# The doubling levels of the delta rule: each 128-column product as two column tiles of 64

## The chip, the cores and the metric

One NeuronCore of a Trainium2 chip (trn2) runs the whole program. The metric is the device time of one execution in microseconds. Engines are called by their names: TensorE (PE in the profile, PEld for its weight loads), VectorE (DVE), ScalarE (ACT), GpSimd (POOL), SyncE (SP).

## What is computed

The reference is one layer of a hybrid encoder for 512 tokens of 1024 channels, in fp32: a layer norm, a mixer with three branches, and a mixture of experts with 32 experts. The change lies in branch (A), the gated delta rule in both directions, 4 heads of 128 channels. In the reference it goes chunk by chunk:

```
m = where(strict, einsum(kb, k) * decay, 0)
a_mat = m + eye
sol = triangular_solve(a_mat, [v * beta, kb * exp(gc)])
...
v_new = u_n - w_n @ state
state_next = state * exp(gl_n) + kd_n^T @ v_new
```

The kernel uses chunks of 128 tokens. It inverts the unit triangular matrix a_mat itself: first its diagonal blocks of 8 by 8, and then by doubling, with blocks of 8, 16, 32 and 64 joined to blocks of twice the size. Joining blocks costs two products for each level, direction, chunk and head: Y = (off-diagonal part) times (inverse so far), and T = T - (inverse so far) times Y.

## The kernel before, in words

The program has four parts with a barrier of all engines between them: `front` (norm, input projection, gates), `mlstm`, `deltanet`, and `back` (merging of the branches, output projection, router, experts).

`deltanet` (from line 1034) treats 8 batches, m = 0 to 7: two directions by four chunks of 128 tokens. Batches 2p and 2p+1 (called a and b) are worked side by side, one of each direction. The order of the steps is written out by hand in the list `order` (lines 1098 to 1124) and each engine walks the same list. For each pair and each of the four levels l it has: y1(a), y1(b), some steps of other batches, p2(a), p2(b), and, but for the last level, again(a), again(b). Step "y1" multiplies the masked matrix `ot` by half of the columns of `tn` (64 of 128, those of one side of each block) into the lower half of the PSUM bank `lv[d]`; ScalarE copies this to `y1s` (line 1440). Step "p2" multiplies `y1s` by half of the columns of `tt` into the upper half of the same bank; VectorE subtracts it from `tt` (line 1547). Step "again" transposes `tt` afresh (line 1323) and ScalarE writes `tn` (line 1436). GpSimd clears `y1s` and masks the next `ot` (lines 1604 and 1608). Line 1289 is the product that solves the 8 by 8 blocks; it waits for VectorE's line 1520.

Between these steps `order` puts matmuls that don't belong to the delta rule: the list `fill` (lines 1128 to 1144), products of the merge gates (line 1250, 128 stationary columns, 512 streamed, split fp32r, three products for each block) and of the other branches (line 1259, plain fp32). They are dealt out by the dictionary `weight`: as the weights of the steps add up, a like share of the fill list is inserted. The weight of y1, p2 and again counts only for odd m, so that a and b follow directly on one another and fill comes behind b. All fill belongs to this part; at its end the engines meet at the barrier, and `back` starts with its loads.

In the program a product is one call. In the trace a plain fp32 product is two weight loads and two matmuls, so the 4 heads of one y1 step are 8 pairs. The two edited lines are 1308 ("y1") and 1316 ("p2").

Two other lines are spoken of for their shape: line 2176 in `back` adds up a small table with 64 stationary columns (8 products, 32 streamed columns), and line 1886 is the second product of the experts, 64 stationary columns and 512 streamed. Lines 1858 and 1859 are the experts' first products with the full 128 columns.

Of the kernel before, what the change touches and what calls it, by code (L numbers as in the profile page):

```python
# [1033 lines left out]
def deltanet(nc, sem, sb, pb, cn, v):  # L1034
# [9 lines left out]
    with st:  # L1044
# [3 lines left out]
        mt, tt, tn, at, qe = (four(name, 4) for name in ("mt", "tt", "tn", "at", "qe"))  # L1048
        ot, rhs = four("ot", 2), four("rhs", 2)
# [6 lines left out]
        y1s = four("y1s", 2)  # L1056
# [15 lines left out]
        lv = [pb(st, f"lv{i}") for i in range(2)]  # L1072
# [85 lines left out]
        def halves(ap, l, side):  # L1158

            return ap.rearrange("p h (n s b) -> p h n s b", s=2, b=LEVELS[l])[:, :, :, side, :]  # L1160

        def packed(bank, part, l):

            return bank[:, 256 * part:256 * part + 256].rearrange("p (h n b) -> p h n b", h=NH, b=LEVELS[l])
# [27 lines left out]
        with nc.Block() as block:  # L1192
# [47 lines left out]
            def _(pe):  # L1240
                for op in order:
                    if op[0] == "fill":
                        what, c, r, k = op[1:]
                        if what == "gate":
# [4 lines left out]
                            for a, b in PRODUCTS:  # L1249
                                last = pe.matmul(fill_bank(what, c, r)[:, :], gw_part[g % 2][a][:, k, :], h_part[b][:, k, :],  # L1250
                                                 start=(k == 0 and a + b == 0), stop=(k == KT - 1 and a == 1))
# [12 lines left out]
                    d, t = BATCH[m]  # L1264
                    tri = cn("upto" if d == 0 else "after")
                    if kind == "gram":
                        if m >= 1:
                            pe.wait_ge(at_ready, m)
                            pe.wait_ge(kk_used, m)
                        if m % 2 == 0 and m >= 2:  # L1270
                            pe.wait_ge(tn_copied, m)
                        for h in range(NH):
                            last = pe.matmul(pr[0][:, tile(h)], gg[:, t, 4 * d + h:4 * d + h + 1].to_broadcast([P, P]), tri,
                                             start=True, stop=True)
                        last.then_inc(gr_done, 1)
                        for h in range(NH):
                            last = pe.matmul(pr[1][:, tile(h)], qkT[:, 1, h, tile(t)], qkT[:, 1, h, tile(t)],
                                             start=True, stop=True)
                        last.then_inc(kk_done, 1)
                    elif kind == "attn":  # L1280
                        pe.wait_ge(dif_ready, m + 1)
                        pe.wait_ge(egr_ready, m + 1)
                        for h in range(NH):
                            last = pe.matmul(pr[0][:, tile(h)], qkT[:, 1, h, tile(t)], qkT[:, 0, h, tile(t)],
                                             start=True, stop=True)
                        last.then_inc(qk_done, 1)
                    elif kind == "base":
                        pe.wait_ge(spread, m + 1)
                        pe.matmul(pr[1][:, :], cn("block"), facts[:, 0:2 * NH * BASE * BASE],
                                  start=True, stop=True).then_inc(base_done, 1)  # L1290
                    elif kind == "turn":
                        pe.wait_ge(tt_ready, m + 1)
                        if m % 2 == 1:
                            pe.wait_ge(tn_copied, m)
                        for h in range(NH):
                            last = pe.transpose(pr[1][:, tile(h)], tt[:, m % 4, h, :], ident)
                        last.then_inc(turn_done, 1)
                    elif kind == "y1":
                        l = op[2]
                        i = at_level(m, l)  # L1300
                        pe.wait_ge(ot_ready, i + 1)
                        pe.wait_ge(tn_copied, m + 1)
                        if i >= 2:
                            pe.wait_ge(t_updated, i - 1)
                        if l > 0:
                            pe.wait_ge(again_copied, at_again(m, l - 1) + 1)
                        for h in range(NH):
                            last = pe.matmul(packed(lv[d], 0, l)[:, h], ot[:, i % 2, h, :],  # L1308
                                             halves(tn[:, m % 4, :, :], l, d)[:, h], start=True, stop=True)
                        last.then_inc(y1_done, 1)  # L1310
                    elif kind == "p2":
                        l = op[2]
                        pe.wait_ge(y1_copied, at_level(m, l) + 1)
                        pe.wait_ge(y1_cleared, at_level(m, l) + 1)
                        for h in range(NH):
                            last = pe.matmul(packed(lv[d], 1, l)[:, h], y1s[:, d, h, :],  # L1316
                                             halves(tt[:, m % 4, :, :], l, 1 - d)[:, h], start=True, stop=True)
                        last.then_inc(p2_done, 1)
                    elif kind == "again":
                        l = op[2]  # L1320
                        pe.wait_ge(t_updated, at_level(m, l) + 1)
                        for h in range(NH):
                            last = pe.transpose(lv[d][:, tile(h)], tt[:, m % 4, h, :], ident)  # L1323
                        last.then_inc(again_done, 1)
                    elif kind == "norm":
                        n = m - NB // 2
                        pe.wait_ge(osq_done, n + 1)
                        pe.wait_ge(o_taken, m + 1)
                        if m < NB - 2:
                            pe.wait_ge(s_updated, m + 1)  # L1330
                        for h in range(NH):
                            last = pe.matmul(sc[m % 2][:, h:h + 1], mt[:, m % 4, h, :], ones[:, 0:1], start=True, stop=True)
                        last.then_inc(osum_done, 1)
                    elif kind == "root":
                        n = m - NB // 2
                        pe.wait_ge(orec_done, n + 1)
                        for h in range(NH):
                            last = pe.matmul(sc[m % 2][:, tile(h)], root_col[:, n, h:h + 1].to_broadcast([P, P]), ident,
                                             start=True, stop=True)
                        last.then_inc(ospread_done, 1)  # L1340
                    elif kind == "read":
                        if m >= 2:
                            pe.wait_ge(s_updated, m - 1)
                        else:
                            pe.wait_ge(s_zero, m + 1)

                        if m >= NB // 2 + 2:
                            pe.wait_ge(ospread_used, m - NB // 2 - 1)
                        for h in range(NH):
                            last = pe.matmul(sc[m % 2][:, tile(h)], qkT[:, 1, h, tile(t)], state[:, d, h, :],  # L1350
                                             start=True, stop=True)
                        last.then_inc(ks_done, 1)
                    elif kind == "solve":
                        pe.wait_ge(r_ready, m + 1)
                        pe.wait_ge(t_updated, at_level(m, NL - 1) + 1)
                        for h in range(NH):
                            last = pe.matmul(sc[m % 2][:, tile(h)], tt[:, m % 4, h, :], rhs[:, d, h, :], start=True, stop=True)
                        last.then_inc(tr_done, 1)
                    elif kind == "write":
                        pe.wait_ge(vn_ready, m + 1)  # L1360
                        pe.wait_ge(at_ready, m + 1)
                        pe.wait_ge(qe_ready, m + 1)
                        for h in range(NH):
                            pe.matmul(sc[m % 2][:, tile(h)], vn[:, d, h, :], at[:, m % 4, h, :], start=True, stop=False)
                            last = pe.matmul(sc[m % 2][:, tile(h)], state[:, d, h, :], qe[:, m % 4, h, :], start=False, stop=True)
                        last.then_inc(o_done, 1)
                        if m < NB - 2:
                            pe.wait_ge(o_taken, m + 1)
                            for h in range(NH):
                                last = pe.matmul(sc[m % 2][:, tile(h)], kTok[:, t, h, :], vnd[:, d, h, :], start=True, stop=True)  # L1370
                            last.then_inc(ds_done, 1)
# [1233 lines left out]
```

## Time and profile before

| | |
|---|---|
| Time, median of 3 runs | 1304.32 us (1302.6 to 1304.48) |
| Span of the profiled execution, first to last instruction | 1295.8 us |
| Median above that span | 8.5 us |
| TensorE busy | 1218.8 us, 94% |
| TensorE weight loads busy | 854.9 us, 66% |
| VectorE, ScalarE, GpSimd busy | 788.6, 618.9, 171.6 us |
| Mean granted TensorE clock | 0.983 |
| Delta rule stage | 270 to 617 us |

The page has no time of its own for the profiled execution beyond its span; the runs shown are separate executions, and the last rows of the table put the two side by side. "Busy" counts matmuls from start to a modelled end, and since matmuls overlap, the distance between their starts tells more than their length. In the timeline one row stands for successive instructions of one line: its start, the time from the first start to the last end, and their number (x). The shape 128*64 means 128 rows and 64 stationary columns; what is behind it is the streamed operand.

### The profile page before, as it was taken

The numbers are of one execution on the slowest core, as the hardware profiler recorded it, in microseconds if no ns is written. First come the engines' busy times: TensorE is split into PE (matmuls) and PEld (weight loads), VectorE is DVE, ScalarE is ACT, GpSimd is POOL, SyncE is SP. The second block draws the span as 40 slices with busy tenths as digits, with TensorE's granted clock in tenths as the row PEclk, the third lists the DMA queues.
The fourth block names the chain that finished last, engine by engine and source line by source line (L and its number), as shares of the span: only waits on it lengthen the run. The fifth ranks groups of instructions, "written<-read, shape, count | busy, mean of one in ns | idle before, by whom it ended". The sixth has DMA issues, their size and how long they took to land.

```text
span 1295.8 us, 14828 instructions
## 1 busy us (share of the span) xinstructions
PE 1218.8 (94%) x5610; PEld 854.9 (66%) x5610; DVE 788.6 (61%) x999; ACT 618.9 (48%) x815; POOL 171.6 (13%) x178
## 2 busy tenths in 40 slices
PE   5999998989999999999897699999999999999996
PEld 4788876767778787877376555666666665555552
DVE  6687753764343444424655667766666666666676
ACT  6354445664324233232322455666666666666652
POOL 1000160022223123120000110111111111111000
PEclk9999999999999999999999699999999999999999
DMA  7323421162212202211935799999999999999951
GB/s 248 99 72 106 148 66 41 35 220 70 76 42 66 81 27 72 65 42 57 336 126 210 269 410 344 385 405 400 405 404 403 397 399 400 401 392 396 397 212 67
DMA packets 98175, 284.72 MB, mean 220 GB/s; under 512 B 8917, under 2 KB 58709, under 8 KB 72880
## 3 DMA queue, kind: packets, MB, share of 16 engines
q1 hardware_dynamic: 92992, 274.94, 56.5%
q0 software_dynamic: 4960, 8.22, 1.9%
q8 instruction: 48, 0.79, 0.3%
q10 hardware_dynamic: 144, 0.52, 0.1%
q14 instruction: 31, 0.25, 0.1%
HBM read 269.13 MB, written 22.56 MB: 225 GB/s over the span
## 4 chain that ended last, share of the span: by engine, by line
PE 68%; DVE 5%; issue 2%; ACT 2%; DMA 1%; SPq 0%; POOLq 0%; ACTq 0%; DVEq 0%
PE yb L1886 17%; PE fill_ps L1250 10%; PE hb L1858 9%; PE hb L1859 9%; PE fill_ps L1259 3%; PE tx L1842 2%; PE hb L2118 2%; PE lv L1308 2%; PE lv L1316 2%; PE gb L1873 1%; PE gb L1866 1%; PE yb L2118 1%; DMA wraw<-kept_dram 1%; PE lv L1323 1%; DVE wo_lo L2280 1%
## 5 line engine op out<-in xcount | busy, mean ns | idle before, releaser
L1979 DVE TENSOR_TENSOR wlo<-wraw,whi 128x2048 fp32r<-128x2048 f32 x127 | 285.4, 2287 | 30.3 <-ACT whi L1920 30.3
L1920 ACT ACTIVATE whi<-wraw 128x2048 fp32r<-128x2048 f32 x128 | 241.1, 1909 | 35.3 <-PE hb L1859 35.3
L1886 PE MATMUL yb<-wraw,act_t 128*64 128x512 f32 x512 | 227.8, 598 | 6.0 <-issue 6.0
L1858 PE MATMUL hb<-whi,xs 128*128 128x512 f32 x512 | 211.8, 414 | 1.8 <-DVE xs L1983 1.5
L1859 PE MATMUL hb<-wlo,xs 128*128 128x512 f32 x512 | 202.5, 396 | 0.0
L1886 PEld LDWEIGHTS yb<-wraw,act_t 128*64 128x64 f32 x512 | 67.8, 137 | 140.6 <-issue 138.8
L1250 PE MATMUL fill_ps<-h_part,gws 128*128 128x512 f32 x576 | 158.5, 416 | 1.8 <-DVE gws L1472 1.8
L1858 PEld LDWEIGHTS hb<-whi,xs 128*128 128x128 f32 x512 | 97.6, 191 | 45.8 <-issue 25.7
L369 PE MATMUL pj<-h_part,wsplit 128*128 128x512 f32 x528 | 126.0, 397 | 0.0
L1250 PEld LDWEIGHTS fill_ps<-h_part,gws 128*128 128x128 f32 x576 | 104.6, 191 | 27.0 <-issue 5.5
L1946 ACT ACTIVATE ys<-yb 64x512 f32<-64x512 f32 x64 | 34.3, 586 | 174.4 <-PE yb L1886 174.4
L369 PEld LDWEIGHTS pj<-h_part,wsplit 128*128 128x128 f32 x528 | 98.9, 188 | 24.5 <-issue 3.4
L1859 PEld LDWEIGHTS hb<-wlo,xs 128*128 128x128 f32 x512 | 97.4, 190 | 18.1
L1989 DVE TENSOR_REDUCE s<-gb 128x256 f32<-128x512 f32 x32 | 22.1, 691 | 120.9 <-PE gb L1866 117.3
L1812 POOL DMA_INDIRECT y_dram<-ys,rows_all x30 | 27.7, 922 | 445.5 <-ACT ys L1946 429.9
L1472 DVE TENSOR_TENSOR gws<-h,gws 128x1024 fp32r<-128x1024 f32 x24 | 31.3, 1307 | 55.8 <-ACT gws L1384 55.8
L1259 PE MATMUL fill_ps<-yT,h 128*128 128x512 f32 x128 | 60.3, 596 | 0.0
L1608 POOL TENSOR_TENSOR ot<-mt,cst 128x512 f32<-128x512 f32 x32 | 43.0, 1343 | 0.0
L1842 PEld LDWEIGHTS tx<-cst,xg 64*128 64x128 f32 x256 | 30.6, 199 | 17.2 <-issue 11.0
L1842 PE MATMUL tx<-cst,xg 64*128 64x64 f32 x256 | 35.1, 278 | 6.0 <-DMA xg<-h_dram,rows_all 6.0
L699 DVE SCALAR_TENSOR_TENSOR cv<-raw,sml,cv 128x512 f32<-128x512 f32 x48 | 36.1, 752 | 1.7
L1806 POOL DMA_INDIRECT xg<-h_dram,rows_all x32 | 31.4, 981 | 36.2 <-DVE rows_all L2414 16.2
(410 smaller groups left out, 1744.8 us busy)
## 6 DMA issues: line engine op xcount, KB each, us to landing
wraw<-in_moe_w SPq DMA_DIRECT2D x192, 1024.0 KB, 11.2
h<-in_w_in SPq DMA_DIRECT2D x24, 512.0 KB, 4.9
kTok<-in_w_in SPq DMA_DIRECT2D x6, 1024.0 KB, 5.5
vTok<-in_w_in SPq DMA_DIRECT2D x6, 1024.0 KB, 5.6
h<-in_w_in SPq DMA_DIRECT2D x4, 1024.0 KB, 5.6
h<-in_w_branch SPq DMA_DIRECT2D x16, 256.0 KB, 2.8
y_dram<-state SPq DMA_DIRECT2D x8, 512.0 KB, 6.6
kept_dram<-h SPq DMA_DIRECT2D x16, 256.0 KB, 2.1
```

Source lines behind the costliest of these rows:

```text
L369: last = pe.matmul(pj[n % 3][:, :], w_part[c % 2][a][:, k, m * P:(m + 1) * P], h_part[b][:, k, :], start=(k == 0 and a + b == 0), stop=(k ...
L699: ins = dve.scalar_tensor_tensor(cv[:, n % 3, :], raw[:, n % 3, j:j + SEQ], taps[:, j:j + 1], cv[:, n % 3, :], ALU.mult, ALU.add)
L1250: last = pe.matmul(fill_bank(what, c, r)[:, :], gw_part[g % 2][a][:, k, :], h_part[b][:, k, :], start=(k == 0 and a + b == 0), stop=(k == ...
L1259: last = pe.matmul(fill_bank(what, c, r)[:, :], bw[b % 2][:, k, :], yT[:, r, k, :], start=(k == 0), stop=(k == NH - 1))
L1608: pool.tensor_tensor(ot[:, i % 2, :, :], mt[:, m % 4, :, :], bc(cn(f"level{d}_{LEVELS[l]}"), 1, NH), ALU.mult).then_inc(ot_ready, 1)
L1842: last = pe.transpose(tx[:, k * SLOTS:(k + 1) * SLOTS], xg[:, e % 2, k::KT], ident[0:SLOTS, 0:SLOTS])
L1858: pe.matmul(bank[:, :], lhs, whi[:, u % NSPLIT, cols], start=(half == 0 and kk == 0), stop=False)
L1859: last = pe.matmul(bank[:, :], lhs, wlo[:, u % NSPLIT, cols], start=False, stop=(half == 1 and kk == 3))
L1886: last = pe.matmul(yb[c][0:SLOTS, :], act_t[:, k, :], raw[:, room, cols], start=(k == 0), stop=(k == FT - 1))
L1920: act.activation(whi[:, u % NSPLIT, :], raw[:, room, :], ACT.Copy).then_inc(S.hi_done.sem, 1)
L1979: dve.tensor_tensor(wlo[:, u % NSPLIT, :], raw[:, room, :], whi[:, u % NSPLIT, :].bitcast(F32), ALU.subtract).then_inc(S.lo_done.sem, 1)
L2118: last = pe.matmul(yp[n % 3][:, :], merged_part[a][:, k, t * P:(t + 1) * P], wo_part[b][:, half, k, :], start=(k == 0 and a + b == 0), sto ...
```

## The change

In both steps the loop over the heads gets an inner loop over two sides. Each call takes 64 of the 128 stationary columns and writes 64 of the 128 output partitions. The streamed operand is the same for both. The order, the semaphores (one signal behind the last call) and all other engines stay.

```
                         for h in range(NH):
-                            last = pe.matmul(packed(lv[d], 0, l)[:, h], ot[:, i % 2, h, :],
-                                             halves(tn[:, m % 4, :, :], l, d)[:, h], start=True, stop=True)
+                            for side in range(2):
+                                rows = slice(64 * side, 64 * side + 64)
+                                last = pe.matmul(packed(lv[d][rows, :], 0, l)[:, h], ot[:, i % 2, h, rows],
+                                                 halves(tn[:, m % 4, :, :], l, d)[:, h], start=True, stop=True)
                         last.then_inc(y1_done, 1)
...
                         for h in range(NH):
-                            last = pe.matmul(packed(lv[d], 1, l)[:, h], y1s[:, d, h, :],
-                                             halves(tt[:, m % 4, :, :], l, 1 - d)[:, h], start=True, stop=True)
+                            for side in range(2):
+                                rows = slice(64 * side, 64 * side + 64)
+                                last = pe.matmul(packed(lv[d][rows, :], 1, l)[:, h], y1s[:, d, h, rows],
+                                                 halves(tt[:, m % 4, :, :], l, 1 - d)[:, h], start=True, stop=True)
                         last.then_inc(p2_done, 1)
```

## Rows read from the trace of the kernel before

**Rows 1.** The page: busy time by engine, and shares of the chain that ended last.

```profile
PE 1218.8 (94%) x5610; PEld 854.9 (66%) x5610; DVE 788.6 (61%) x999; ACT 618.9 (48%) x815; POOL 171.6 (13%) x178
...
PE 68%; DVE 5%; issue 2%; ACT 2%; DMA 1%; SPq 0%; POOLq 0%; ACTq 0%; DVEq 0%
```

**Rows 2.** Table by stage; its first row names the columns, (x) counts instructions.

```profile
core 0: us, PE busy (x) PEld busy (x) DVE busy (x) ACT busy (x) POOL busy (x), PEclk, DMA share, GB/s
...
270.00:617.00 347.00, 332.23 (x1913) 268.06 (x1914) 153.52 (x260) 119.41 (x197) 78.67 (x80) 1.00 0.25 74
617.00:745.00 128.00, 107.28 (x452) 76.39 (x452) 75.33 (x126) 39.38 (x45) 6.90 (x6) 0.89 0.63 238
745.00:1272.00 527.00, 520.25 (x1999) 310.29 (x1998) 363.98 (x298) 314.60 (x308) 53.98 (x58) 1.00 0.96 378
```

**Rows 3.** Whom TensorE waited for in 270 to 617: total us, times, longest.

```profile
PE sc L1370 <- ACT oT L1444: 2.7, 4, 0.7
PE pr L1289 <- DVE facts L1520: 2.7, 2, 1.6
PE sc L1332 <- ACT mt L1450: 2.5, 2, 2.1
```

**Rows 4.** Groups of 270 to 617, then one line's min/median/max ns.

```profile
L1308 PE MATMUL lv<-tn,ot 128*128 128x64 f32 x256 | 30.4, 272 | 0.3 <-ACT tn L1436 0.3
L1316 PE MATMUL lv<-tt,y1s 128*128 128x64 f32 x256 | 30.3, 272 | 0.0
...
L1316 PEld LDWEIGHTS lv<-tt,y1s 128*128 128x128 f32 x256 | 31.0, 192 | 3.3 <-issue 2.4
L1308 PEld LDWEIGHTS lv<-tn,ot 128*128 128x128 f32 x256 | 31.0, 192 | 3.5 <-issue 2.5
...
L1308 PE MATMUL lv<-tn,ot x256: 217/275/294, 304.2 to 567.0; 128*128 128x64 f32 x128
```

**Rows 5.** Timeline around one L1308 stretch: start us, length us, engine, line.

```profile
303.96 0.39 PE L1250 MATMUL fill_ps<-h_part,gws 128*128 128x512 f32 x1
304.20 0.33 PE L1308 MATMUL lv<-tn,ot 128*128 128x64 f32 x2
...
303.97 0.42 PEld L1308 LDWEIGHTS lv<-tn,ot 128*128 128x128 f32 x2
...
305.31 0.64 PEld L1308 LDWEIGHTS lv<-tn,ot 128*128 128x128 f32 x5
305.87 0.54 PEld L1250 LDWEIGHTS fill_ps<-h_part,gws 128*128 128x128 f32 x3
...
306.22 0.39 PE L1250 MATMUL fill_ps<-h_part,gws 128*128 128x512 f32 x1
```

**Rows 6.** Timeline around L2176 (64 stationary columns), and its min/median/max ns.

```profile
777.17 0.40 PE L1858 MATMUL hb<-whi,xs 128*128 128x512 f32 x1
777.40 0.39 PE L1859 MATMUL hb<-wlo,xs 128*128 128x512 f32 x1
...
777.17 0.19 PEld L1859 LDWEIGHTS hb<-wlo,xs 128*128 128x128 f32 x1
777.72 1.01 PEld L2176 LDWEIGHTS cp<-cst 128*64 128x64 f32 x16 [0.36 <-issue]
...
L2176 PEld LDWEIGHTS cp<-cst x16: 133/138/138, 777.7 to 778.6; 128*64 128x64 f32 x16
...
778.41 0.31 PEld L2176 LDWEIGHTS cp<-cst 128*64 128x64 f32 x4
778.77 0.19 PEld L1858 LDWEIGHTS hb<-whi,xs 128*128 128x128 f32 x1
...
778.77 0.50 PE L1858 MATMUL hb<-whi,xs 128*128 128x512 f32 x1
779.11 0.40 PE L1859 MATMUL hb<-wlo,xs 128*128 128x512 f32 x1
```

**Rows 7.** Timeline at the end of an L1886 block, and its group on the page.

```profile
771.95 1.45 PE L1886 MATMUL yb<-wraw,act_t 128*64 128x512 f32 x3
773.33 0.50 PE L1858 MATMUL hb<-whi,xs 128*128 128x512 f32 x1
...
773.32 0.19 PEld L1858 LDWEIGHTS hb<-whi,xs 128*128 128x128 f32 x1 [0.81 <-issue]
...
L1886 PE MATMUL yb<-wraw,act_t 128*64 128x512 f32 x512 | 227.8, 598 | 6.0 <-issue 6.0
```

**Rows 8.** Timeline of TensorE after the L1308 stretch at 348.6.

```profile
348.61 1.89 PE L1308 MATMUL lv<-tn,ot 128*128 128x64 f32 x16
...
353.10 1.12 PE L1289 MATMUL pr<-facts,cst 128*128 128x512 f32 x2 [1.15 <-DVE facts L1520]
```

## The prediction

> **What bounds the kernel now.** I began with the page: TensorE is busy in 94% of the span, and the chain that ended last is TensorE for 68% [rows 1]. The table by stage then says where that matters here. The delta rule runs from 270 to 617 us; in it TensorE is busy for 332.2 of 347 us at the full clock, while the DMA engines are busy a quarter of the time and VectorE for less than half [rows 2]. So this stage is as long as TensorE's own list of work. After it comes a barrier (all engines leave the block), and then the expert stage, which is at 0.96 of the DMA engines [rows 2]. It loads its weights only after the barrier, so it starts later or earlier by what the delta rule loses or wins, and gives nothing back. I take a microsecond of TensorE time in this stage for a microsecond of the whole.
>
> TensorE's waits in the stage are few: the longest sums are 2.7, 2.7 and 2.5 us [rows 3]. The two edited lines have 256 matmuls and 256 weight loads each, from 128 products each (an fp32 product is two loads and two matmuls), and wait for almost nothing [rows 4].
>
> **How one such product is paid for.** The order puts y1(a), y1(b) behind each other, and p2(a), p2(b) too: 8 products, 16 pairs of load and matmul, with fill products or other whole-array work on both sides. There are 16 stretches of each line, 32 in all. In one of them the loads follow at (0.64 - 0.192) / 4 = 0.112 us, for 128 stationary columns [rows 4, 5]. The matmul itself, 64 columns streamed, needs far less: the first two of the stretch, whose loads are there early, start 0.33 - 0.275 = 0.055 us apart [rows 4, 5]. So **the load is the price**, not the product: 0.112 us a pair, whatever is streamed behind it.
>
> Such a stretch, from the start of the last fill matmul before it (303.96) to the start of the second one after it (306.22), takes 2.26 us [rows 5]. Its edges are cheap, because the first load is issued at 303.97 beneath the running fill matmul, and the next fill's load beneath the last products [rows 5].
>
> **The change, part by part.** Each product becomes two, with the same 64 streamed columns and 64 stationary ones each, written to partitions 0 to 63 and 64 to 127. Loads and matmuls of the two lines double to 512 each per line; a stretch has 32 pairs. No wait, semaphore, buffer or DMA is added; the last matmul still gives the only signal. So the whole cost is on TensorE.
>
> *Pairs.* The trace has one place with 64 stationary columns and a short stream: L2176, 16 loads in 1.01 us, so (1.01 - 0.14) / 15 = 0.058 us each [rows 6]. It streams 32 columns and not 64, but 0.055 us for 64 is still less than the load. All of L2176 lies in the same columns of the array, though; a place where two column tiles alternate doesn't exist in this trace. If loads stay one behind the other, a stretch has 31 x 0.058 = 1.80 us between its first and last load, against 16 pairs of 0.112 = 1.79 us now: **halving the columns halves the load, and doubling the number gives it back.**
>
> *Edges.* In the same rows the last full matmul before L2176 starts at 777.40 and the first load of L2176 only at 777.72, 0.32 us later. A full one takes about 0.23 us (777.17 to 777.40), so the engine ran empty for 0.09 us, and the load wasn't pulled ahead [rows 6]. Behind it, the last load of L2176 is at 778.41 + 3 x 0.058 = 778.59, the next full load at 778.77, and the second full matmul at 779.11, because the first one starts together with its load [rows 6]. That this isn't a semaphore of L2176 I take from L1886, also 64 columns wide: its matmuls are spaced at (1.45 - 0.598) / 2 = 0.43, so the last one starts at 772.81 and makes room at 773.24; the next full load comes at 773.32, again 0.09 late, and not ahead [rows 7]. The Trainium skill says the same under TensorEngine Tiling (Array Packing), Key Properties: changing the tiling mode drains the TensorE. The trace agrees, with 0.09 us a side.
>
> *Sum for a stretch.* 0.32 (entry) + 1.80 (31 loads) + 0.52 (778.59 to 779.11) + 0.03 (64 streamed columns at the end instead of 32) = 2.67 us, against 2.26. That is +0.41 us, times 32 = **+13.1 us**. Of it, one wait takes some back: the product of the base blocks at 353.10 waits 1.15 us for VectorE, and VectorE doesn't depend on the L1308 stretch that ends at 350.3 [rows 8]; TensorE coming 0.4 us later just waits less. I subtract 0.4: **+12.7 us**. The other long waits (L1370, L1332) follow directly on the step that they wait for and stay.
>
> *Unknown cost, both bounds.* The pair in two alternating tiles is the unknown. From below: if the two tiles load at the same time, two pairs cost 0.058, so 0.029 each. From above: if a load can't run beneath the other tile's matmul, each change of tile adds the matmul's 0.055. I take 0.058, by the nearest row, L2176, which has the same width and the same type. A second argument is the density of instructions: its loads and matmuls already follow at 0.029 us per instruction, and I saw nothing denser in the trace; overlap of the tiles would need 0.015.
>
> *Span and median.* 1295.8 + 12.7 = 1308.5 us of span. The median of the runs, 1304.32, is 8.5 us above the span of the profiled execution (the page gives no other time for that execution); I carry the 8.5 over: **1317.0 us**.
>
> **The rivals.**
>
> *The tiles load side by side (faster).* Place: within the 32 stretches. Two loads go in the time of one, 31 loads take 0.90 instead of 1.80 us, the edges stay: 1.77 us a stretch, 0.49 less than now, times 32 = -15.7; the wait at 353 us grows by 0.5. Result 1304.3 - 15.2 = 1289.1 us. It decides from the point at which a load costs less than (1.80 - 0.41) / 31 = 0.045 us, so already a fifth of overlap turns the sign. For it: the two halves use different columns and different output partitions, and nothing in the data ties them. Against it: no row shows it, and the density of instructions above. The Trainium skill, in the same section, has this as a rule: tiles operate independently, and different tiles can load and multiply in parallel. By that rule the result would be this rival's; the trace of before can't confirm it. Chance 0.30.
>
> *A load waits for the other tile's matmul (much slower).* The tile changes after every two pairs, 15 times a stretch; 15 x 0.055 = 0.82 us more than in my sum, 1.23 a stretch, 39 in all: 1343 us. For it there is only that each load of L1308 that runs early today does so within one set of columns. The Trainium skill has a sentence that way, in TensorE: Matmul & The Clock Gate, Part 3, The mechanism: loads overlap with matmuls in flight only when the row group differs, and the two tiles here share their rows. The trace speaks against it as a general rule, since loads of the same rows do run ahead [rows 5]. Chance 0.08.
>
> *It isn't a tile at all.* If the engine treats a product of 64 columns as a narrow one of the whole array, there is no drain: 32 x 0.058 = 1.86 against 1.79, +0.07 a stretch, +2.1 us, 1306.4. L2176 and L1886 speak against it. Chance 0.06. A partial overlap that just pays for the edges lands around 1304 too: 0.06, half of it in the band, a quarter on each side.
>
> **How the numbers follow.** My forecast, loads one behind the other with drained edges, has 0.50; its own range is 1312 (drains half hidden) to 1322 (one more drain of about 0.16 us a stretch, where the second batch waits for its own semaphore). A measurement of this kernel can tell 0.2%, 2.6 us, from no change. With the case of partial overlap split as said, slower is 0.50 + 0.08 + 0.015, rounded to 0.59; within is 0.06 + 0.03, rounded up to 0.10; faster is 0.30 + 0.015, rounded to 0.31. Forecast and no-tile case together hold 0.56, too little for 8 in 10, so the range goes down to the faster rival: 1288 to 1322. That leaves out the much slower one and the tails. Cases of both signs hold the most; the likeliest one's own range is 1312 to 1322.
>
> **What would show it.** In the profile of the changed kernel: 512 loads and 512 matmuls on each of the two lines, with 64 columns and a mean load near 138 ns instead of 192; the spacing of the loads in a stretch, 0.058 for me, 0.029 for the first rival, about 0.085 for the second; the first load of a stretch about 0.09 us behind the end of the fill matmul, and the first fill matmul after it starting with its load. From the last fill matmul to the second after it I expect 2.67 us. The stage should end near 630 us, the barrier's wait and everything after it unchanged in length, the wait of L1289 shorter. I am wrong if the distance between loads is below 0.045 us, or if the edges show no gap; and the step from stage to whole is wrong if the expert stage shrinks or grows by more than a microsecond.

## The result, and the profile after

The changed kernel takes 1288.2 us in the median (1282.89 to 1292.27, 4 runs), the kernel before 1304.4 us beside it (4 runs): a ratio of 0.9895, 95% interval 0.9868 to 0.9922. It is **faster by about 1%**. I had forecast 1317.0 and slower. 1288.2 lies 0.9 us from the rival "the tiles load side by side", 1289.1, and only just inside the range, whose low end was 1288. The interval of the ratio, applied to 1304.4, runs from 1287.2 to 1294.2.

First the page after, its rows on busy time and on the chain (answering to [rows 1]):

```profile
PE 1210.0 (94%) x6122; PEld 832.3 (65%) x6122; DVE 787.7 (61%) x999; ACT 618.4 (48%) x815; POOL 173.3 (13%) x178
...
PE 67%; DVE 5%; issue 2%; ACT 2%; DMA 1%; SPq 0%; POOLq 0%; ACTq 0%; DVEq 0%
```

There are 512 more matmuls and 512 more loads, as said, and TensorE is busy for less time. The groups of the delta rule stage (answering to [rows 4]; the two lines are now 1310 and 1320):

```profile
L1310 PE MATMUL lv<-tn,ot 128*64 128x64 f32 x512 | 18.4, 225 | 0.3 <-ACT tn L1440 0.3
L1320 PE MATMUL lv<-tt,y1s 128*64 128x64 f32 x512 | 18.4, 225 | 0.0
...
L1310 PEld LDWEIGHTS lv<-tn,ot 128*64 128x64 f32 x512 | 16.3, 138 | 7.7 <-issue 7.7
L1320 PEld LDWEIGHTS lv<-tt,y1s 128*64 128x64 f32 x512 | 16.2, 138 | 7.6 <-issue 7.5
```

Twice the instructions are busy for 18.4 us a line where it was 30.4. 512 loads of 138 ns would be 71 us end to end; that the group is busy for 16.3 us says that they lie over one another. The same stretch as in [rows 5], from the timeline after:

```profile
308.37 0.63 PE L1250 MATMUL fill_ps<-h_part,gws 128*128 128x512 f32 x2
308.93 1.15 PE L1310 MATMUL lv<-tn,ot 128*64 128x64 f32 x32
...
308.93 1.01 PEld L1310 LDWEIGHTS lv<-tn,ot 128*64 128x64 f32 x32 [0.37 <-issue]
...
310.34 0.39 PE L1250 MATMUL fill_ps<-h_part,gws 128*128 128x512 f32 x1
```

32 loads in 1.01 us: less the last one's own 0.14, 31 steps of 0.028 us. (L2176 needed the same 1.01 us for 16 loads of the same width [rows 6].) The last fill matmul before starts at 308.60 (the row's end, 309.00, less 0.39), the second after at 310.34: 1.74 us against 2.26. The edges are there as forecast: the first load comes 0.33 us behind the start of the last fill matmul, and no load is ahead of it.

The stage runs from the first start of line 1273 to the first start of the barrier's next product (2101 before, 2105 after). Both, before and then after, from the views of the lines:

```profile
L1273 PE MATMUL pr<-cst,gg x64: 270/274/347, 270.2 to 491.8; 128*128 128x128 f32 x64
...
L2101 PE MATMUL hb<-yT,h x48: 592/592/697, 616.8 to 646.2; 128*128 128x512 f32 x48
```

```profile
L1273 PE MATMUL pr<-cst,gg x64: 271/274/422, 274.8 to 486.9; 128*128 128x128 f32 x64
...
L2105 PE MATMUL hb<-yT,h x48: 592/592/697, 606.3 to 635.3; 128*128 128x512 f32 x48
```

Exactly: 346.6 us before, 331.4 us after, so **15.2 us less in this stage**. The span is only 8.2 us shorter (1295.8 to 1287.6), because the parts that the change doesn't touch were longer in this profiled execution: the front by 4.6 us, the experts (from the second product of the first one to the end) by 2.6, while the part between was 0.2 shorter. Both go with a lower granted clock. The front, in the table by stretches, before and then after:

```profile
180.00:290.00 110.00, 99.58 (x511) 1.00 0.28 93
```

```profile
180.00:290.00 110.00, 99.98 (x489) 0.95 0.24 77
```

Over all profiles taken, the front was 269.8 to 271.2 us long in some and 274.0 to 276.0 in others; the changed kernel itself had 274.8, 275.7 and 269.9. The experts took 550.0 to 550.2 us or 552.8 to 553.4 us. The first group is the profile before, experiments 3 and 5 and one of the two of four tiles, the second all the others, the slower kernel of experiment 2 among them. In their first 85 us the mean granted clock was 0.98 before and 0.94 after. That is why I compare stages and stretches in the experiments, and whole times only by their intervals.

The stage has such a place too, and it bears on the comparisons below. From the last matmul of the last p2 step to the end of the stage the kernels have the same work on TensorE, but for a few fill products in experiment 6. This tail took 46.6 to 46.8 us in most profiles, the one before and the first two of the changed kernel among them, and 45.2 to 45.4 in four: the third of the changed kernel and experiments 3, 4 and 6. The table by stretches for that tail, before, after, in the third profile of the changed kernel and in experiment 3:

```profile
570.20:616.84 46.64, 42.65 (x229) 0.96 0.17 57
```

```profile
559.52:606.25 46.73, 42.74 (x233) 0.96 0.18 57
```

```profile
554.59:599.78 45.19, 41.20 (x234) 1.00 0.18 59
```

```profile
572.53:617.74 45.21, 41.23 (x229) 1.00 0.18 59
```

A stretch at the lower level (1.2 GHz) is in some tails and not in others, and is worth 1.5 us. So the stages of experiments 3, 4 and 6 are to be compared with the 329.9 us of the third profile of the changed kernel, and the others with 331.4.

### The profile page after: what moved, and what is told of

It is laid out like the page before. It is cut to its first block, busy times and chain, and to the rows that moved or that the text cites. A ratio compares the mean times of both kernels' runs of the same rounds, so it can differ in the third digit from the quotient of the medians.

```text
span 1287.6 us, 15852 instructions
## 1 busy us (share of the span) xinstructions
PE 1210.0 (94%) x6122; PEld 832.3 (65%) x6122; DVE 787.7 (61%) x999; ACT 618.4 (48%) x815; POOL 173.3 (13%) x178
## 4 chain that ended last, share of the span: by engine, by line
PE 67%; DVE 5%; issue 2%; ACT 2%; DMA 1%; SPq 0%; POOLq 0%; ACTq 0%; DVEq 0%
PE yb L1890 18%; PE fill_ps L1250 10%; PE hb L1862 9%; PE hb L1863 9%; PE fill_ps L1259 4%; PE tx L1846 2%; PE hb L2122 2%; PE lv L1310 1%; PE lv L1320 1%; PE gb L1877 1%; PE gb L1870 1%; PE yb L2122 1%; DMA wraw<-kept_dram 1%; PE lv L1327 1%; DVE wo_lo L2284 1%
## 5 line engine op out<-in xcount | busy, mean ns | idle before, releaser
L1890 PE MATMUL yb<-wraw,act_t 128*64 128x512 f32 x512 | 230.9, 605 | 6.0 <-issue 6.0
L1810 POOL DMA_INDIRECT xg<-h_dram,rows_all x32 | 31.5, 983 | 36.2 <-DVE rows_all L2418 16.8
```

What stands on the lines that cost most here:

```text
L1890: last = pe.matmul(yb[c][0:SLOTS, :], act_t[:, k, :], raw[:, room, cols], start=(k == 0), stop=(k == FT - 1))
```

## Experiments

Each stage length below is measured as above. "Stretch" is the median over the 16 stretches of a line, from the last fill matmul before to the second matmul after; it was 2.25 us before and 1.75 after. Summed over all 32 stretches, that is 75.6 us before and 59.2 after, 16.4 less. The theory at this point was the rival that had come true: two column tiles load and multiply side by side. Against it stood that narrow loads might be cheap for another reason, and that part of the gain was scatter.

**1. The change again.** No edit.

> The changed kernel once more, for its stretches and for how far the parts outside the delta rule scatter. Theory (two column tiles load and multiply side by side): delta rule stage 331 us again (346.6 before), a stretch of 32 pairs 1.75 us from the last fill matmul before it to the second after it (2.26 before). The rest of the program is the same as before apart from scatter of a few us. Rival (part of the gain was scatter): the stage differs from 331 by more than 2 us.

Measured: stage 331.4 us, stretch 1.747 us; 1288.19 us, ratio 0.9886 (0.9857 to 0.9915). A third time, beside the last two experiments:

> The changed kernel beside the two below, on the same chip and against the same runs of the kernel before: delta rule stage 331.4 us, ratio 0.988 to 0.990.

Measured: stage 329.9 us (with the full clock in the tail), stretch 1.747 us; 1285.31 us, ratio 0.9882 (0.9860 to 0.9904). The gain in the stage is real and repeats; of the third profile's 16.8 us below the kernel before, 1.5 are the clock's.

**2. The same instructions in one tile.** This isolates the step at which I had gone wrong. The kernel leaves out the upper half of each product, so it doesn't compute the layer.

```
-                                last = pe.matmul(packed(lv[d][rows, :], 0, l)[:, h], ot[:, i % 2, h, rows],
+                                last = pe.matmul(packed(lv[d][0:64, :], 0, l)[:, h], ot[:, i % 2, h, rows],
...
-                                last = pe.matmul(packed(lv[d][rows, :], 1, l)[:, h], y1s[:, d, h, rows],
+                                last = pe.matmul(packed(lv[d][0:64, :], 1, l)[:, h], y1s[:, d, h, rows],
...
+                    dve.memset(lv[d][:, :], 0.0).then_inc(lv_zero, 1)
```

> Both halves of each product of y1 and p2 are written to partitions 0 to 63, so that all narrow products lie in one column tile; the upper half of each product is left out (those partitions hold zeros or older values), and VectorE clears the two banks once. Same number of loads and matmuls as the change. Theory (the gain comes from neighbouring instructions in different tiles): the loads follow at 0.058 us, 31 of them take 1.80 us, with the measured edges of 0.82 us a stretch is 2.62 us, the stage 331.4 + 32 x 0.87 = 359 us, the time some 12 us above the kernel before. Rival (a narrow load is cheap whatever tile it goes to): 1.75 us and 331 us.

Measured: stage 358.9 us; 1316.01 us, ratio 1.0093 (1.0060 to 1.0126). Its first stretch:

```profile
307.75 0.63 PE L1250 MATMUL fill_ps<-h_part,gws 128*128 128x512 f32 x2
308.31 2.08 PE L1312 MATMUL lv<-tn,ot 128*64 128x64 f32 x32
...
308.31 1.94 PEld L1312 LDWEIGHTS lv<-tn,ot 128*64 128x64 f32 x32 [0.37 <-issue]
```

Same count, same width, and 32 loads take 1.94 instead of 1.01 us: (1.94 - 0.14) / 31 = 0.058 us each. The stretch is 2.67 us. What differs in the program (VectorE's two clears at the start and one wait for them apart) is where the second half goes. With it two more things differ: the values, since the upper halves hold zeros or older ones, and that both halves are now written to the same place. Neither is the cause: in experiment 3, with the right values and a place of its own for every head, the loads within one tile also follow at 0.058 us. The clock isn't either, the tail had 0.96 here as before. The gain comes from two tiles being used, and not from narrow loads.

**3. The two loops swapped.**

```
-                        for h in range(NH):
-                            for side in range(2):
+                        for side in range(2):
+                            for h in range(NH):
```

> The two loops are swapped: all four heads in the lower tile, then all four in the upper one, so that the tile changes 3 times in a stretch instead of 15. Theory A (side by side only where neighbouring instructions go to different tiles): the loads follow at 0.058 us within a side, a stretch takes about 2.5 to 2.67 us, the stage 355 to 360 us, the time 8 to 13 us above the kernel before. Theory B (each tile draws its instructions from its own queue, far ahead): a stretch stays near 1.75 us and the stage near 331.

Measured: stage 341.8 us, stretch 2.13 us; 1298.91 us, ratio 0.9986 (0.9975 to 0.9997). The stage lies about halfway between the two theories:

```profile
310.08 1.54 PE L1310 MATMUL lv<-tn,ot 128*64 128x64 f32 x32
...
310.08 1.40 PEld L1310 LDWEIGHTS lv<-tn,ot 128*64 128x64 f32 x32 [0.37 <-issue]
```

1.40 us for the loads lies between 1.01 and 1.94. At each of the 3 changes of tile (1.94 - 1.40) / 3 = 0.18 us is saved, about three loads of 0.058. The single starts say the same: counted from the first load of this stretch, the sixth load of the lower tile starts at 0.286 us and the first one of the upper tile at 0.288, ahead of the lower tile's seventh (0.344) and eighth. So the engine does look ahead past a tile that is held, but only over a few instructions; the tiles don't work off whole lists of their own. The 32 stretches take 71.6 us, so 4.0 of the 16.4 us are left: the order of the calls is worth some 12 us. The stages say so too, 341.8 against 329.9.

**4. Two heads in a tile, then the same two in the other.** To test that reading.

```
-                        for h in range(NH):
-                            for side in range(2):
+                        for pair, side, one in [(a, b, c) for a in range(2) for b in range(2) for c in range(2)]:
+                            if True:
+                                h = 2 * pair + one
```

> Two heads in the lower tile, the same two in the upper one, then the next two: the tile changes 7 times in a stretch (15 in the change, 3 with the loops swapped, where each change hid 0.16 us of loads). Theory (the engine looks some three loads ahead, past a tile that is held): 7 x 0.16 us would be more than the 0.87 us there is to gain, so the stretch is 1.75 to 1.9 us. Rival (only the one load at the change is hidden, 0.058 us each): 2.6 - 7 x 0.058 = 2.2 us.

Measured: stretch 1.79 us, stage 331.3 us; 1289.55 us in a single run.

```profile
308.74 1.06 PEld L1311 LDWEIGHTS lv<-tn,ot 128*64 128x64 f32 x32 [0.37 <-issue]
```

With four pairs to a tile before it changes, the 32 loads take 1.06 us, nearly the 1.01 of two pairs. A look ahead of about three loads explains this and experiment 3; hiding one load a change would have given 2.2 us a stretch. The stage isn't as short as the change's: its tail had the full clock, so it stands beside 329.9 us, 1.5 longer, as 32 x 0.046 us would have it.

**5. Only y1 in two tiles.** Line 1320's product as before.

```
-                            for side in range(2):
-                                rows = slice(64 * side, 64 * side + 64)
-                                last = pe.matmul(packed(lv[d][rows, :], 1, l)[:, h], y1s[:, d, h, rows],
-                                                 halves(tt[:, m % 4, :, :], l, 1 - d)[:, h], start=True, stop=True)
+                            last = pe.matmul(packed(lv[d], 1, l)[:, h], y1s[:, d, h, :],
+                                             halves(tt[:, m % 4, :, :], l, 1 - d)[:, h], start=True, stop=True)
```

> Only step y1 is made in two tiles, p2 is as before. If the gain is 0.51 us a stretch, 16 stretches give 8.2 us: stage 338.5 us, time about 1296. If one of the two steps held the gain by its own wait (y1 by ScalarE's copy, p2 by VectorE's subtraction), it would be near 0 or near 15.

Measured: stage 338.9 us, that is 7.7 less than before and 7.5 more than the change; 1294.38 us, ratio 0.9949 (0.9931 to 0.9966). The two steps share the gain evenly. It is TensorE time, and no wait of ScalarE or VectorE behind one of them.

**6. Twice as many edges.** Fill products also between a and b.

```
-        slot = lambda op: weight[op[0]] if op[1] % 2 == 1 or op[0] not in ("y1", "p2", "again", "read", "solve", "write") else 0.0
+        slot = lambda op: weight[op[0]] / 2 if op[0] in ("y1", "p2") else weight[op[0]] if op[1] % 2 == 1 or op[0] not in ("again", "read", "solve", "write") else 0.0
```

> The weight of y1 and p2 is given to even and odd batches alike, half each, so that fill products come between a and b as well: 64 stretches of 16 pairs instead of 32 of 32. Theory (each change to tiles and back costs the measured edges): a stretch of 16 pairs takes 0.82 + 0.45 = 1.27 us; two of them 2.53 against 1.75 + 0.47 for the fill matmuls counted twice, +0.32 us a split, 32 splits, +10 us: stage 341 to 342 us. Rival (edges are hidden by the long fill matmuls): stage within 2 us of 331.4.

Measured: 64 stretches of 1.28 us, stage 341.8 us; 1299.99 us, ratio 0.9991 (0.9973 to 1.0009). A split costs 2 x 1.28 - 1.75 - 0.47 = 0.34 us, 11 us for all 32, and beside the 329.9 us of the same clock the stage is 11.9 longer, where the sum had said 10. The edges alone take back more than two thirds of the gain. The order with more splits wasn't run on the kernel before, so how much of the last microsecond is the order's own stays open.

```profile
308.25 0.63 PE L1250 MATMUL fill_ps<-h_part,gws 128*128 128x512 f32 x2
308.81 0.69 PE L1310 MATMUL lv<-tn,ot 128*64 128x64 f32 x16
309.43 0.96 PE L1250 MATMUL fill_ps<-h_part,gws 128*128 128x512 f32 x3
310.32 0.69 PE L1310 MATMUL lv<-tn,ot 128*64 128x64 f32 x16
```

Each stretch comes out and in again by a fill matmul that starts with its own load: from 309.43 the three fill matmuls hold the engine for 0.89 us, where three in a row elsewhere take 0.70.

**7. Tiles where 128 columns are streamed.** The products of gram and attn too.

```
+                def two(out, lhsT, rhs, start, stop):
+                    for side in range(2):
+                        rows = slice(64 * side, 64 * side + 64)
+                        last = pe.matmul(out[rows], lhsT[:, rows], rhs, start=start, stop=stop)
+                    return last
...
-                            last = pe.matmul(pr[0][:, tile(h)], gg[:, t, 4 * d + h:4 * d + h + 1].to_broadcast([P, P]), tri,
+                            last = two(pr[0][:, tile(h)], gg[:, t, 4 * d + h:4 * d + h + 1].to_broadcast([P, P]), tri,
...
-                            last = pe.matmul(pr[1][:, tile(h)], qkT[:, 1, h, tile(t)], qkT[:, 1, h, tile(t)],
+                            last = two(pr[1][:, tile(h)], qkT[:, 1, h, tile(t)], qkT[:, 1, h, tile(t)],
...
-                            last = pe.matmul(pr[0][:, tile(h)], qkT[:, 1, h, tile(t)], qkT[:, 0, h, tile(t)],
+                            last = two(pr[0][:, tile(h)], qkT[:, 1, h, tile(t)], qkT[:, 0, h, tile(t)],
```

> On top of the change, the products of gram and attn (128 streamed columns) are made in two column tiles too. Theory (tiles pay only where the load is longer than the stream): each tile is held by its own matmuls of 0.109 us, so 16 pairs' worth still takes 1.74 us (1.79 before), and 16 new stretches pay 0.18 us of edges: stage 2 to 3 us longer than 331.4. Rival (side by side halves any product): 8 x 0.9 + 8 x 0.45 us less, 2.9 more for edges: stage 8 us shorter, 323.

Measured: stage 338.5 us, 7.1 longer than the change; 1295.99 us in a single run. The sign was right and the size too small. A gram step (8 + 8 pairs in whole products) first in the change, from the profile of experiment 1, then here:

```profile
337.50 1.05 PE L1273 MATMUL pr<-cst,gg 128*128 128x128 f32 x8
338.39 1.06 PE L1277 MATMUL pr<-qkT 128*128 128x128 f32 x8
339.29 1.88 PE L1259 MATMUL fill_ps<-yT,h 128*128 128x512 f32 x4
```

```profile
339.98 1.10 PE L1244 MATMUL pr<-cst,gg 128*64 128x128 f32 x16
340.91 1.04 PE L1244 MATMUL pr<-qkT 128*64 128x128 f32 x16
341.88 1.98 PE L1265 MATMUL fill_ps<-yT,h 128*128 128x512 f32 x4
```

From its first matmul to the fill behind it: 1.79 us with whole products, 1.90 in tiles. Nothing is won inside: each tile's matmuls follow at 0.109 us, held by their own stream of 128 columns. The edges cost 0.31 us a gram stretch and 0.33 an attn stretch, and not 0.18. In tiles the first fill matmul starts 0.20 us behind the last gram matmul (its stream of 0.109 and about 0.09 again), and in whole products it started 0.03 behind it, its load fully hidden; behind y1 it was 0.15 in tiles and 0.08 whole. 16 stretches make 5.1 us. In the rest are a stretch of the lower clock at 298 us, which the change's profile doesn't have, and a wait of L1289's product for VectorE at 297.6, 2.20 us against 1.55.

**8. Four tiles of 32.**

```
-                            for side in range(2):
-                                rows = slice(64 * side, 64 * side + 64)
+                            for side in range(4):
+                                rows = slice(32 * side, 32 * side + 32)
```

> Each product as four column tiles of 32, so 64 pairs a stretch. Theory (loads and matmuls of different tiles run side by side without a limit of issue): a load of 32 columns is then shorter than the 0.055 us matmul, each tile is held by its 16 matmuls of 0.056 us, 0.9 us in all, as much as two tiles take: stretch 1.70 to 1.75 us, stage 331. Rival (two tiles are already at the rate at which instructions can be issued, 0.0146 us each): 128 instructions take 1.87 us, a stretch 2.7 us, and the stage gets some 14 us longer than before, 360 us.

Measured: stretch 1.694 us, stage 330.0 us; 1285.07 us, ratio 0.9880 (0.9856 to 0.9905).

```profile
305.28 1.10 PE L1310 MATMUL lv<-tn,ot 128*32 128x64 f32 x64
...
305.28 0.94 PEld L1310 LDWEIGHTS lv<-tn,ot 128*32 128x32 f32 x64 [0.37 <-issue]
```

64 matmuls and 64 loads in about 0.9 us are 0.007 us an instruction. So issue limits nothing here. The bound has passed from the loads to the matmuls: each tile has 16 matmuls of 64 streamed columns, and 16 of 0.055 us are 0.88 us. In one tile the loads follow at 0.056 us here, and at 0.032 us where only 32 columns are streamed (experiment 9), so it isn't the loads that hold them at 0.056. Once more, beside the next one:

> Four column tiles of 32 once more: stage 330.0 us, 1.4 us less than with two tiles (32 stretches at 1.694 instead of 1.747 us). The time is 1 to 2 us below that of two tiles, which the measurement may not tell from none.

Measured: stage 330.1 us, stretch 1.694 us; 1282.71 us, ratio 0.9854 (0.9830 to 0.9877), against 0.9882 for two tiles in the same session. The intervals overlap; the traces say 0.053 us a stretch, 1.7 us in all. The stage of the changed kernel in that session, 329.9 us, is no counterexample: it had the full clock in the tail, and both profiles of four tiles had 0.96.

**9. Four tiles in the router's products too.** They stream 32 columns with 128 stationary ones, in the part behind the barrier.

```
-                        last = pe.matmul(lp[:, t * NE:(t + 1) * NE], hT[:, k, t * P:(t + 1) * P], wc[:, k, :],
-                                         start=(k == 0), stop=(k == KT - 1))
+                        for side in range(4):
+                            rows = slice(32 * side, 32 * side + 32)
+                            last = pe.matmul(lp[rows, t * NE:(t + 1) * NE], hT[:, k, t * P + 32 * side:t * P + 32 * side + 32], wc[:, k, :],
+                                             start=(k == 0), stop=(k == KT - 1))
```

> Four tiles in y1 and p2, and the router's products in the part after the barrier (four groups of 8 products of 32 streamed columns, now 1.59 us between first and last matmul, three times the full clock) in four column tiles too. Theory (tiles pay wherever the load is longer than the stream): a group falls to about 0.5 us, with 0.18 to 0.3 us of edges, so 0.7 to 0.9 us less each for those on the path, 3 us in all: from the barrier to the first expert 125.5 instead of 128.5 us, the time 3 us below four tiles. Rival (the experts' first weights are what is waited for there): 128.5 us as before.

Measured: 1280.96 us, ratio 0.9854 (0.9832 to 0.9877), the lowest median of all kernels here. A group without the edit (profile of the repeat in experiment 8), then with it:

```profile
666.19 1.87 PE L2142 MATMUL tx<-small_a,h2T 128*128 128x32 f32 x16
667.89 0.47 PE L2122 MATMUL yb<-wo_hi,merged_hi 128*128 128x512 f32 x1
```

```profile
662.07 0.76 PE L2144 MATMUL tx<-small_a,h2T 128*32 128x32 f32 x64
662.77 0.51 PE L2122 MATMUL yb<-wo_hi,merged_hi 128*128 128x512 f32 x1
```

1.70 us becomes 0.70. With the edges, a group on the path costs 0.89 us less. From the first product behind the barrier to the start of the first expert's first product it takes 107.4 us instead of 110.1 in the repeat of four tiles, 2.7 less, which is three groups; to the start of its second product 125.1 instead of 127.1 (128.5 in their first run), so 0.7 is lost again in between. 3 us were expected. That the whole is faster than with four tiles in the delta rule alone is likely by the traces, and not shown by the times: the ratio is the same.

## Why the prediction was wrong, point by point

**The failed step** is the one on the unknown cost: "I take 0.058, by the nearest row, L2176". The row was right for what it shows, products in one tile. Experiment 2 builds just that, and there the sum holds: forecast 2.67 us a stretch, measured 2.67; the wait of L1289 forecast 0.4 shorter, measured 0.74 against 1.15; forecast +12.7 us for the stage and the whole, measured 358.9 - 346.6 = +12.3 in the stage and a ratio of 1.0093. But the change alternates between two tiles, and there a load costs 0.028 us, the low bound of 0.029 that I had named and set aside. I chose between two ends far apart by a row that differed in the one property that mattered. That a fifth of overlap would turn the sign also made the rival look nearer than it was: it is a fifth off the price of a load, 0.058 to 0.045, and nearly half of the way to 0.029.

**The second argument failed too.** I had held against the rival that nothing denser than 0.029 us per instruction stood in the trace. That was the spacing of the loads within one tile, and no limit of issue: four tiles reach 0.007 us.

**Right:** that the load and not the stream is the price of these products; the edges (0.87 us a stretch in the sum, 0.82 in the trace: 0.33 in, 0.49 out, which counts from the last matmul where the sum counts from the last load), which experiment 6 bears out; that only this stage changes. The wait of the base product did grow as the rival said:

```profile
354.66 1.12 PE L1289 MATMUL pr<-facts,cst 128*128 128x512 f32 x2 [1.63 <-DVE facts L1524]
```

1.63 us against 1.15 in [rows 8].

**Not in the sum.** Two more waits for VectorE grew, that of an "again" step and that of the transposes of line 1296. Before and then after, for each:

```profile
423.18 0.44 PE L1323 MATMUL lv<-cst,tt 128*128 128x128 f32 x2 [0.62 <-DVE tt L1547]
```

```profile
421.50 0.44 PE L1327 MATMUL lv<-cst,tt 128*128 128x128 f32 x2 [0.92 <-DVE tt L1551]
```

```profile
443.81 0.44 PE L1296 MATMUL pr<-cst,tt 128*128 128x128 f32 x2 [0.42 <-DVE tt L1535]
```

```profile
441.41 0.44 PE L1296 MATMUL pr<-cst,tt 128*128 128x128 f32 x2 [0.71 <-DVE tt L1539]
```

The three together took back 0.5 + 0.3 + 0.3 = 1.1 us of the 16.4 that the stretches gained, which leaves 15.3; the stage shows 15.2. The rival's sum was 15.7 less 0.5. So that it names the stage's 15.2 to the tenth is luck, two small errors that cancel, and so is the 0.9 us between its 1289.1 and the measured 1288.2, since the times scatter by more.

**The two cited rules.** The rule that tiles operate independently (the Trainium skill, TensorEngine Tiling (Array Packing), Key Properties) was the one to trust; the change and experiment 2 agree with it, 1.01 us against 1.94 for as many loads of the same width. The sentence on loads beneath matmuls only where the row group differs (the Trainium skill, TensorE: Matmul & The Clock Gate, Part 3, The mechanism) doesn't hold here: the tiles share their rows, and the loads of one run beside the loads and matmuls of the other, 0.028 us apart on average with a load of 0.138 us.

**Span and median.** I carried 8.5 us from the span to the median. Every profiled execution with a time of its own lies 1.8 to 1.9 us above its span (1289.5 and 1287.6 for the changed kernel). The other 6.6 us were scatter: the profiled execution before was one of the short ones. This did no harm, because carrying it over is the same as adding the change to the median before. The kernel before came out at 1300.8 to 1302.1 us in the medians of the later sessions, so the gain of the whole is 13 to 16 us. I had also said that the step from the stage to the whole is wrong if the expert stage changes by more than a microsecond. It grew by 2.6, but with the granted clock, and both lengths occur with one and the same kernel, four tiles (553.3 and 550.0 us). All three profiles of the changed kernel had the longer one, so that the change brings it on more often isn't excluded.

**The chances.** 0.50 for my case against 0.30 for the rival was too much for a choice that the trace didn't decide: no row showed two tiles in alternation.

## What to carry to other kernels

Where a product streams fewer columns than its stationary operand takes to load, compute the price from the distance between loads, and split the stationary columns over tiles that alternate from call to call; here 128 stationary and 64 streamed columns in fp32 gained 43% between the edges (1.62 to 0.93 us), and 128 streamed columns gained nothing. Count the changes between tiles and whole-array work first, 0.18 to 0.33 us for the way in and back out together, and keep tiled products together. When a cost is bounded from two sides and the nearest row lacks the very property in question, build the sum for both ends and don't let nearness choose. Before two stages are compared to the microsecond, look at the granted clock in a part that didn't change.

## What I had not expected of the hardware

- Loads for two column tiles that share all rows run side by side: 0.028 us each where 0.058 is the price in one tile.
- The look ahead past a held tile is short: about three loads (0.18 us a change of tile when the tile changes every 8 pairs), so the order of calls decides. Runs of 8 pairs to a tile keep a quarter of what 2 pairs gain in the stretches (4.0 of 16.4 us), runs of 4 nearly all (15.0).
- TensorE took 128 loads and matmuls in 0.9 us, 0.007 us each, and in experiment 9 in under 0.6, 0.0045 each. With four tiles most neighbouring loads started 6 to 7 ns apart in the first, and some closer in the second; where the limit of issue lies wasn't reached or tested.
- The same change to tiles costs more behind a longer stream (0.31 us a gram stretch against 0.18 for y1): the tile's longer last stream has to end first, and there the next load had been hidden before.
